# Two gates of the first pair as seven half-wide products, h's sums from x brought again, attention's last blocks earlier

## The chip, the cores and the metric

The kernel runs on one core of one Trainium2 chip. The metric is the device time of one execution in microseconds, the median of several runs.

## The reference

One layer of a hybrid encoder trunk, batch 1, sequence S = 512, D = 2048, float32 in and out. `x` is normalised (RMSNorm with a gain) to `h`; one projection `z = h @ W_in` feeds four mixers: A a gated MLP over blocks of 128 positions, B sliding-window attention (8 query heads, 2 key/value heads, width 64, chunks of 64), C trailing means, D a gated convolution of 31 taps. Each mixer is projected to D and multiplied by a sigmoid gate of `h`. An output projection, a residual, and a SwiGLU with its own norms follow.

```python
h = rms_norm(x, norm_mix_pre[l])
z = h @ w_in[l]
...
merged = jax.nn.sigmoid(h @ w_gate[l, 0] + b_gate[l, 0]) * y_a
merged = merged + jax.nn.sigmoid(h @ w_gate[l, 1] + b_gate[l, 1]) * y_b
merged = merged + jax.nn.sigmoid(h @ w_gate[l, 2] + b_gate[l, 2]) * y_c
merged = merged + jax.nn.sigmoid(h @ w_gate[l, 3] + b_gate[l, 3]) * y_d
x = x + rms_norm(merged @ w_o[l], norm_mix_post[l])
h2 = rms_norm(x, norm_ffn_pre[l])
gu = h2 @ w_ffn_in[l]
f = (jax.nn.silu(gu[..., :D_FF]) * gu[..., D_FF:]) @ w_ffn_out[l]
x = x + rms_norm(f, norm_ffn_post[l])
```

## The kernel before, in words

**Layout and precision.** Activations lie transposed: features on the 128 partitions in tiles, the 512 positions along the free dimension. Every matrix product is made of float16 matmuls on a high and a low part of both factors, three matmuls for one: high x high, high x low, low x high. ScalarE makes the high part of a weight unit by a Copy (`hi`, L630), VectorE the low part as weight minus high part (`lo`, L1121). A unit is 128x1024 weights (512 KB), brought by SP into one of 8 stage slots; the two parts go to one of 4 ring slots (`wq`). So `load(q)` waits until the low part of the unit that had the stage slot is made, and `hi(u)` waits until the products of the unit four before are done. The normalisation factor of `h` is applied after the product, when a bank is emptied, so `h` itself is stored as x times the gain in two float16 parts.

**Order of the work.** There are 13 chunks of W_in (n = 0 to 12; four units each, 52 in all; from chunk 2 on they are copied as a whole, `hi_chunk` L638 and `lo_chunk` L1128). A chunk is two output tiles, each of two units and 48 matmuls of 512 columns. Then come the gates: eight pairs jj of output tiles, and in each pair four gates j = 0 to 3 for the branches D, B, A, C. Behind each gate's product stands the branch's own projection (`branch`, one unit, 24 matmuls; for C six), and VectorE's `merge` multiplies it by the sigmoid and adds up. Every engine runs its own instruction stream in the order in which the code is written; semaphores join them.

**Plain gates and product gates.** A plain gate is two tiles of two units (`plain_tile`, L1969 to L1971). It is used for pair 0, for all four j. Pairs 1 to 7 use Strassen's scheme: four quarter units of weights and their sums (`make_s3`, `make_s2`, `make_s1`, `make_s4` on VectorE) give seven products of half width (`product`, L1976 to L1978: 24 matmuls of 256 columns each) into banks Q1 to Q4. ScalarE keeps three of the results (`keep_product`, L826), VectorE adds them (`c22_c21` L1159 and L1160, `c12_c11`), and the next products wait for these by `copied` and `c_read`.

**The sums of h.** The products need four sums of quarters of `h` for each of the eight pairs of tiles (`tset`). `h_sums(i)` adds the two float16 parts of the pair again (L1500, 128x1024), then makes four steps of 128x256 (L1169 to L1175), ScalarE takes the high part (`t_high`, L787) and VectorE the low part (`h_t_low`, L1179). Two buffers `t_h` take turns. In pair 0 the sums of tiles 0 to 2 are made in gate j=0, 3 to 5 in j=1, 6 and 7 in j=2. TensorE waits for `t_lo` = 8 before the first product gate.

**Tasks.** Small work is hung between the big products by a number k: `tasks(2n)` and `tasks(2n+1)` of chunk n on ScalarE and VectorE; TensorE does task 2n+1 after the first tile of chunk n and task 2n+2 after the second. Gates j = 0 to 3 go on with k = 26 to 33. Attention has four blocks m of 128 positions: scores (TensorE), softmax (VectorE: maximum, shift), exponentials (ScalarE, L694), normalisation (VectorE, L1295 to L1303), transposes of the probabilities (TensorE), their high and low part, heads (TensorE), high and low part of the result (`heads_high` L710, `heads_low` L1323). The tables are

```python
SCORES_AT, NORMALIZE_AT, PROBS_AT, HEADS_AT = (15, 17, 20, 23), (15, 18, 21, 24), (16, 19, 22, 25), (17, 20, 23, 26)
```

Tasks 20 to 23 also transpose the values of mixer A through bank 7, one block of positions each; `value_stats(m)` on VectorE (L1366 to L1370) empties the bank and counts `av_used`, on which the next transposes wait. Task 22 makes the low part of the convolution's output (`d_out`, L1408), task 27 the spatial gating (L1426, L1429) after 16 matmuls (L2190), tasks 27 and 31 the windows of mixer C (L1436), which GpSimd sums (L570 to L578), tasks 28 and 29 the parts of `a_out`, tasks 32 and 33 those of `c_out`. In the gates ScalarE's order for plain gate j is: hi of B+4 and B+5, sigmoid of tile 0 (L800), hi of B+6 and B+7, sigmoid of tile 1 (L809), hi of B+8, where B = `U_G0 + 5*j` is the gate's first unit, B+4 its branch and B+5 the next gate's first. `U_G0` is unit 52.

## Time and profile before

| what | value |
|---|---|
| median of 3 runs | 2445.07 us (2444.79 to 2445.9) |
| the profiled execution | 2445.74 us, its span 2444.0 us |
| TensorE busy | 2422.7 us |
| VectorE busy | 2103.2 us |
| ScalarE busy | 1169.2 us |
| granted TensorE clock | 0.999 |

In the profile's names PE is TensorE, DVE VectorE, ACT ScalarE, POOL GpSimd and SP SyncE, which issues all DMAs. The span is shorter than the execution's time by what lies around it. In a timeline the first number is the start in us from the span's start, the second the duration, and in brackets stands how long the engine had been idle and what released it. Matmuls are pipelined: the duration of one (0.38 us) is longer than the distance to the next, so a group's price is read from the distance between starts. The granted clock stays at its upper level (2.4 GHz) through the span.

### The profile page before, as it was taken

What the parts mean: (1) busy time and instruction counts of PE and PEld (TensorE: products, weight loads), DVE (VectorE), ACT (ScalarE), POOL (GpSimd) and SP (SyncE); (2) the same over time, 40 slices, a digit from 0 to 9 for tenths busy, and PEclk for the clock granted to TensorE, in tenths of its full rate; (3) what the DMA queues carried; (4) which work ended last, traced back from release to release, by engine and by line L of the source; (5) the groups of instructions that cost most, each with busy time, mean ns of one, the idle gap of its engine ahead of it and who ended that gap; (6) DMA issues with size and microseconds to landing.
All of it is one profiled execution on the core that took longest, in us unless ns stands there. A gap on an engine that the chain in (4) does not pass through costs nothing.

```text
span 2444.0 us, 45875 instructions
## 1 busy us (share of the span) xinstructions
PE 2422.7 (99%) x19471; PEld 1893.2 (77%) x19471; DVE 2103.2 (86%) x2292; ACT 1169.2 (48%) x1409; POOL 117.9 (5%) x91
## 2 busy tenths in 40 slices
PE   9999999999999999999899999999999999999998
PEld 5444446888888888768648888888888888888887
DVE  7997588788888888898898999999999998777776
ACT  5235234444444444456564555555555554444443
POOL 0000020000000000011310000000000000000011
PEclk9999999999999999999999999999999999999999
DMA  6222222323333333334333433433433346433436
GB/s 261 104 104 104 73 84 92 120 98 122 114 102 125 106 123 105 132 147 148 113 129 113 138 129 120 138 129 120 138 129 120 137 152 252 143 119 122 136 113 251
DMA packets 97210, 317.94 MB, mean 130 GB/s; under 512 B 9504, under 2 KB 26272, under 8 KB 95648
## 3 DMA queue, kind: packets, MB, share of 16 engines
q1 hardware_dynamic: 97056, 315.81, 37.4%
q8 instruction: 106, 1.74, 0.3%
q14 instruction: 48, 0.39, 0.0%
HBM read 292.18 MB, written 23.59 MB: 129 GB/s over the span
## 4 chain that ended last, share of the span: by engine, by line
PE 88%; DVE 8%; issue 2%; ACT 1%; DMA 1%; POOL 0%; DVEq 0%; SPq 0%; ACTq 0%; POOLq 0%
PE psum L1976 17%; PE psum L1977 17%; PE psum L1978 17%; PE psum L1969 7%; PE psum L1971 7%; PE psum L1970 7%; PE psum L2323 5%; PE psum L2324 5%; PE psum L2325 5%; DVE wq L1121 2%; DVE region_f L1351 1%; DVE region_f L1669 1%; ACT wq L630 1%; DVE region_f L1478 0%; DVE region_f L1489 0%
## 5 line engine op out<-in xcount | busy, mean ns | idle before, releaser
L630 ACT ACTIVATE wq<-stage 128x1024 f16<-128x1024 f32 (+1 forms) x758 | 776.4, 1030 | 685.3 <-DVE stage L1144 277.7
L1121 DVE SCALAR_TENSOR_TENSOR wq<-stage,wq 128x1024 f16<-128x1024 f32 (+1 forms) x758 | 901.4, 1199 | 234.1 <-ACT wq L630 229.5
L1976 PE MATMUL psum<-region_t,wq 128*128 128x256 f16 x2368 | 645.5, 273 | 0.0
L1977 PE MATMUL psum<-region_t,wq 128*128 128x256 f16 x2368 | 645.5, 273 | 0.0
L1978 PE MATMUL psum<-region_t,wq 128*128 128x256 f16 x2368 | 645.5, 273 | 0.0
L1976 PE MATMUL psum<-region_f,wq 128*128 128x256 f16 x1776 | 484.1, 273 | 2.1 <-DVE work L1159 1.8
L1978 PE MATMUL psum<-region_f,wq 128*128 128x256 f16 x1776 | 484.1, 273 | 0.0
L1977 PE MATMUL psum<-region_f,wq 128*128 128x256 f16 x1776 | 484.1, 273 | 0.0
L1969 PE MATMUL psum<-region_f,wq 128*128 128x512 f16 x720 | 272.9, 379 | 0.9 <-DVE wq L1121 0.9
L1970 PE MATMUL psum<-region_f,wq 128*128 128x512 f16 x720 | 272.9, 379 | 0.0
L1971 PE MATMUL psum<-region_f,wq 128*128 128x512 f16 x720 | 272.9, 379 | 0.0
L1977 PEld LDWEIGHTS psum<-region_t,wq 128*128 128x128 f16 x2368 | 231.7, 98 | 26.9
L1976 PEld LDWEIGHTS psum<-region_t,wq 128*128 128x128 f16 x2368 | 231.7, 98 | 26.9
L1978 PEld LDWEIGHTS psum<-region_t,wq 128*128 128x128 f16 x2368 | 231.7, 98 | 26.7
L2323 PE MATMUL psum<-region_f,wq 128*128 128x256 f16 x873 | 238.0, 273 | 1.3 <-DVE wq L1121 1.3
L2325 PE MATMUL psum<-region_f,wq 128*128 128x256 f16 x873 | 238.0, 273 | 0.0
L2324 PE MATMUL psum<-region_f,wq 128*128 128x256 f16 x873 | 238.0, 273 | 0.0
L826 ACT ACTIVATE work<-psum 128x256 f32<-128x256 f32 x222 | 84.9, 382 | 290.4 <-PE psum L1978 253.3
L1976 PEld LDWEIGHTS psum<-region_f,wq 128*128 128x128 f16 x1776 | 173.8, 98 | 27.4 <-DVE wq L1121 3.6
L1977 PEld LDWEIGHTS psum<-region_f,wq 128*128 128x128 f16 x1776 | 173.8, 98 | 23.1
L1978 PEld LDWEIGHTS psum<-region_f,wq 128*128 128x128 f16 x1776 | 173.8, 98 | 20.0
L1971 PEld LDWEIGHTS psum<-region_f,wq 128*128 128x128 f16 x720 | 70.4, 98 | 85.0
(267 smaller groups left out, 2970.0 us busy)
## 6 DMA issues: line engine op xcount, KB each, us to landing
stage<-w_ffn_in_chunks SPq DMA_DIRECT2D x176, 512.0 KB, 3.8
stage<-w_gate_chunks SPq DMA_DIRECT2D x128, 512.0 KB, 3.7
stage<-w_ffn_out_chunks SPq DMA_DIRECT2D x64, 448.0 KB, 3.7
stage<-w_in_chunks SPq DMA_DIRECT2D x52, 512.0 KB, 5.6
stage<-w_o_chunks SPq DMA_DIRECT2D x32, 512.0 KB, 3.8
stage<-w_ffn_out_chunks SPq DMA_DIRECT2D x32, 512.0 KB, 3.8
stage<-w_branch_chunks SPq DMA_DIRECT2D x24, 512.0 KB, 3.5
t_spill<-region_f SPq DMA_DIRECT2D x22, 512.0 KB, 3.2
```

The costliest lines, as they stand in the source:

```text
L630: nc.scalar.activation(dst, stage[:, SLOT[q], 0:UNIT_W[u]], ACT.Copy, scale=WSCALE).then_inc(hi_ready, 1)
L826: nc.scalar.activation(copies[:, i, :], psum[:, Q1, 0:HS], ACT.Copy).then_inc(copied, 1)
L1121: V.scalar_tensor_tensor(out=slot[:, 1, 0:w], in0=stage[:, SLOT[q], 0:w], scalar=WSCALE, in1=slot[:, 0, 0:w], op0=ALU.mult, op1=ALU.subtra ...
L1969: mm(to, w[:, 0, w_at:w_at + P], x_hi, start=start, stop=False)
L1970: mm(to, w[:, 0, w_at:w_at + P], x_lo, start=False, stop=False)
L1971: return mm(to, w[:, 1, w_at:w_at + P], x_hi, start=False, stop=stop)
L1976: mm(to, w[:, 0, w_at:w_at + P], x[:, 0, :], start=start, stop=False, skip_group_check=True)
L1977: mm(to, w[:, 0, w_at:w_at + P], x[:, 1, :], start=False, stop=False, skip_group_check=True)
L1978: return mm(to, w[:, 1, w_at:w_at + P], x[:, 0, :], start=False, stop=stop, skip_group_check=True)
L2323: mm(to, w[:, 0, i * P:i * P + P], xi[:, 0, :], start=first and i == 0, stop=False, skip_group_check=True)
L2324: mm(to, w[:, 0, i * P:i * P + P], xi[:, 1, :], start=False, stop=False, skip_group_check=True)
L2325: done = mm(to, w[:, 1, i * P:i * P + P], xi[:, 0, :], start=False, stop=last and i == n - 1, skip_group_check=True)
```

## The change

- In pair 0 only gates j = 0 and 1 stay plain (`PLAIN_G = 2`); j = 2 and 3 become product gates, with the weights' quarters in that order. All product gates are counted anew by `gate_at`. TensorE waits for `t_lo` = 8 before pair 0's gate j=2.
- `h_sums` no longer adds the two parts of `h`. SP brings the pair of tiles of `x` again into a buffer (`bring_pair`), ScalarE multiplies it in place by the gain (`pair_scaled`), and VectorE makes the four steps from it. Five places serve as buffers for the eight pairs; they lie in the regions of the values, the keys and a free part.
- The sums are made earlier: 0 in chunk 11, 1 to 3 in chunk 12, 4 and 5 in gate j=0, 6 and 7 in gate j=1.
- Attention's blocks 2 and 3 are moved up: scores at 20 and 22, normalisation in the same tasks, probabilities at 21 and 23, heads at 22 and 24. For even tasks ScalarE's exponentials move from `tasks` ahead of the chunk's weight copy.
- Mixer C's last two windows go from task 31 to 29, its high part from 32 to 30, its low part from 33 to 31.

```diff
-PLAIN_O, PLAIN_FFN = 2, 4
+PLAIN_G, PLAIN_O, PLAIN_FFN = 2, 2, 4
...
+def gate_at(jj, j):
+    n = 4 * jj + j - PLAIN_G
+    return U_G + (SU + 1) * n, CS_G + n
...
-SCORES_AT, NORMALIZE_AT, PROBS_AT, HEADS_AT = (15, 17, 20, 23), (15, 18, 21, 24), (16, 19, 22, 25), (17, 20, 23, 26)
+SCORES_AT, NORMALIZE_AT, PROBS_AT, HEADS_AT = (15, 17, 20, 22), (15, 18, 20, 22), (16, 19, 21, 23), (17, 20, 22, 24)
...
-        t_h = view(region_f, O + 2 * b2, 4 * S, F32, "p (u q s) -> p u q s", u=2, q=4)
+        t_h = [view(region_f, i, 2 * S, F32, "p (q s) -> p q s", q=4)
+               for i in (X + 6 * S, O, O + 2 * S, O + 8 * S, O + 10 * S, X + 6 * S, O + 8 * S, O + 10 * S)]
... SP
+            def bring_pair(i):
+                sp.dma_start(t_h[i].rearrange("p (r h) s -> p r (h s)", r=2), x[:, 2 * i:2 * i + 2, :]).then_inc(x_landed[i], 16)
+            def bring_pairs(q):
+                if q == 4 * N_IN + 7:
+                    sp.wait_ge(av_done, NB)
+                    bring_pair(1)
+                    bring_pair(2)
+                    sp.wait_ge(pv_done, NB)
+                    bring_pair(3)
+                    bring_pair(4)
+                if q == 4 * N_IN + 9:
+                    sp.wait_ge(t_lo, 1)
+                    bring_pair(5)
+                if q == 4 * N_IN + 14:
+                    sp.wait_ge(t_lo, 4)
+                    bring_pair(6)
+                if q == 4 * N_IN + 15:
+                    sp.wait_ge(t_lo, 5)
+                    bring_pair(7)
+            sp.wait_ge(h_lo, KT)
+            sp.wait_ge(x_squared, PAIRS)
+            bring_pair(0)
...
                         load(q + i, w_gate[jj, j, i])
+                        bring_pairs(q + i)
... ScalarE
+                if k in SCORES_AT and k % 2 == 0:
+                    exp_part(SCORES_AT.index(k))
...
                     act.wait_ge(au_ready, BT)
+                    act.wait_ge(t_lo, 3)
...
+            def pair_scaled(i):
+                act.wait_ge(x_landed[i], 32)
+                for k in (2 * i, 2 * i + 1):
+                    some = t_h[i][:, 2 * (k % 2):2 * (k % 2) + 2, :]
+                    nc.scalar.activation(some, some, ACT.Copy, scale=vecs[:, V_PRE + k:V_PRE + k + 1]).then_inc(v_made, 1)
...
                 finish(n, 0)
-                if n + 1 == N_IN:
+                if n == N_IN - 1:
+                    act.wait_ge(unit_done, DONE[4 * (N_IN - 2) + 3])
+                    t_high(0)
                     hi(U_G0)
                     hi(U_G0 + 1)
                 attention_highs(2 * n + 1)
                 tasks(2 * n + 1)
+                if n == N_IN - 2:
+                    pair_scaled(0)
+                    pair_scaled(1)
+                if n == N_IN - 1:
+                    pair_scaled(2)
+                    t_high(1)
+                    pair_scaled(3)
                 finish(n, 1)
             hi(U_G0 + 2)
+            t_high(2)
             hi(U_G0 + 3)
... first_gate(j), ScalarE
                 hi(u + 4)
                 col = V_BG + b * KT
+                if j == 0:
+                    pair_scaled(4)
+                    t_high(3)
                 hi(u + 5)
-                if j < 3:
-                    t_high(3 * j)
+                if j == 0:
+                    pair_scaled(5)
+                if j == 1:
+                    t_high(6)
                 act.wait_ge(evicted0, E_G + j + 1)
                 nc.scalar.activation(sig0_0, sig0_0, ACT.Sigmoid, bias=vecs[:, col:col + 1]).then_inc(gate_open, 1)
-                if j < 3:
-                    t_high(3 * j + 1)
                 tasks(k + 1)
+                if j == 0:
+                    t_high(4)
                 hi(u + 6)
+                if j == 0:
+                    pair_scaled(6)
                 hi(u + 7)
-                if j < 2:
-                    t_high(3 * j + 2)
+                if j == 0:
+                    t_high(5)
+                    pair_scaled(7)
+                if j == 1:
+                    t_high(7)
                 act.wait_ge(evicted1, E_G + j + 1)
                 nc.scalar.activation(sig1_0, sig1_0, ACT.Sigmoid, bias=vecs[:, col + 1:col + 2]).then_inc(gate_open, 1)
                 hi(u + 8)
... VectorE, chunk 12
                 if n == N_IN - 1:
+                    h_sums(1)
+                    h_t_low(0)
                     lo(U_G0)
                     lo(U_G0 + 1)
...
+                if n == N_IN - 2:
+                    h_sums(0)
+                if n == N_IN - 1:
+                    h_sums(2)
+                    h_t_low(1)
                 evict(n, 1)
             lo(U_G0 + 2)
+            h_sums(3)
+            h_t_low(2)
             lo(U_G0 + 3)
... VectorE, plain gate j (now for j in range(PLAIN_G))
                 lo(B + 4)
+                if j == 0:
+                    h_sums(4)
+                    h_t_low(3)
+                if j == 1:
+                    h_sums(6)
+                    h_t_low(5)
+                if j == PLAIN_G - 1:
+                    make_s3(U_G, CS_G)
                 lo(B + 5)
...
                 lo(B + 6)
+                if j == 0:
+                    h_t_low(4)
+                    h_sums(5)
+                if j == 1:
+                    h_sums(7)
+                    h_t_low(6)
+                if j == PLAIN_G - 1:
+                    make_s2(U_G, CS_G)
+                    make_s1(U_G, CS_G)
                 lo(B + 7)
+                if j == 1:
+                    h_t_low(7)
... VectorE, product gate
+                if jj == 0:
+                    tasks(2 * (N_IN + j))
...
                 scale_gate(1, 3 * cs + 2)
+                if jj == 0:
+                    tasks(2 * (N_IN + j) + 1)
... TensorE
+                    u, cs = gate_at(0, j)
+                    pe.wait_ge(t_lo, KP)
+                    strassen(h, u, cs, cs == 0)
```

## Rows read from the trace of the kernel before

**Rows 1.** The page: busy time of each engine, and one costly group.

```profile
PE 2422.7 (99%) x19471; PEld 1893.2 (77%) x19471; DVE 2103.2 (86%) x2292; ACT 1169.2 (48%) x1409; POOL 117.9 (5%) x91
...
L630 ACT ACTIVATE wq<-stage 128x1024 f16<-128x1024 f32 (+1 forms) x758 | 776.4, 1030 | 685.3 <-DVE stage L1144 277.7
```

**Rows 2.** What TensorE waited for: us in total, times, longest.

```profile
PE psum L1976 <- DVE work L1159: 1.8, 7, 0.7
```

**Rows 3.** Busy time of each engine in one stretch.

```profile
80.00:398.00 318.00, 318.00 (x1722) 151.31 (x1720) 257.88 (x298) 117.50 (x105) 24.56 (x26) 1.00 0.26 92
```

**Rows 4.** TensorE's timeline, first matmuls of groups, and a last one.

```profile
295.65 0.39 PE L1969 MATMUL psum<-region_f,wq 128*128 128x512 f16 x1
...
309.60 0.38 PE L1969 MATMUL psum<-region_f,wq 128*128 128x512 f16 x1
...
376.94 0.38 PE L1969 MATMUL psum<-region_f,wq 128*128 128x512 f16 x1
...
398.95 0.27 PE L1976 MATMUL psum<-region_f,wq 128*128 128x256 f16 x1
...
414.56 0.27 PE L1978 MATMUL psum<-region_f,wq 128*128 128x256 f16 x1
```

**Rows 5.** VectorE's timeline, tasks 20 to 22.

```profile
228.00 0.69 DVE L1323 TENSOR_TENSOR region_f<-psum,region_f 128x512 f16<-128x512 f32 x1 [1.18 <-ACT region_f L710]
...
231.28 0.69 DVE L1366 BATCH_NORM_STATS2 lnstat<-psum 128x6 f32<-128x512 f32 x1
...
232.88 4.42 DVE L1128 SCALAR_TENSOR_TENSOR region_t<-stage,region_t 128x4096 f16<-128x4096 f32 x1
...
239.01 1.21 DVE L1295 TENSOR_REDUCE rms<-region_t 128x8 f32<-128x1024 f32 x1
...
241.84 0.69 DVE L1366 BATCH_NORM_STATS2 lnstat<-psum 128x6 f32<-128x512 f32 x1
...
252.64 2.28 DVE L1408 TENSOR_TENSOR region_f<-region_f 128x2048 f16<-128x2048 f32 x1
254.84 0.69 DVE L1366 BATCH_NORM_STATS2 lnstat<-psum 128x6 f32<-128x512 f32 x1
```

**Rows 6.** ScalarE's timeline, tasks 20 and 21.

```profile
231.49 1.28 ACT L694 ACT_TABLE_LOAD   x1
...
233.96 1.28 ACT L733 ACT_TABLE_LOAD   x1
...
241.07 1.52 ACT L733 ACTIVATE region_f<-region_f,vecs 128x512 f32<-128x512 f32 x2
242.63 1.91 ACT L738 ACTIVATE region_f<-region_f 128x2048 f16<-128x2048 f32 x1
```

**Rows 7.** ScalarE's groups from 1225 to 1290 us: busy us, mean ns of one.

```profile
L948 ACT ACTIVATE region_f<-region_f,vecs 128x512 f32<-128x512 f32 x16 | 10.4, 708 | 2.5 <-DVE region_t L1179 2.5
```

**Rows 8.** Four loads of SP, issued from 237.3 to 238.7 us.

```profile
DMA to landing us min/median/max: 3.6/5.1/6.4
```

**Rows 9.** VectorE's timeline from chunk 12's end to the end of gate j=0.

```profile
295.59 2.35 DVE L1121 SCALAR_TENSOR_TENSOR wq<-stage,wq 128x1024 f16<-128x1024 f32 x2
...
303.34 1.22 DVE L1500 TENSOR_TENSOR region_f<-region_f 128x1024 f32<-128x1024 f16 x1
304.59 0.43 DVE L1169 TENSOR_TENSOR region_f<-region_f 128x256 f32<-128x256 f32 x1
...
313.23 0.68 DVE L1426 TENSOR_TENSOR region_f<-psum,region_f 128x512 f32<-128x512 f32 x1
...
318.53 1.29 DVE L1436 SCALAR_TENSOR_TENSOR region_f<-work,region_f 128x512 f32<-128x512 f32 x2
...
322.97 1.29 DVE L1169 TENSOR_TENSOR region_f<-region_f 128x256 f32<-128x256 f32 x1
...
328.29 2.05 DVE L1121 SCALAR_TENSOR_TENSOR wq<-stage,wq 128x1024 f16<-128x1024 f32 x1
```

**Rows 10.** GpSimd's timeline, its third window.

```profile
319.82 2.03 POOL L572 TENSOR_TENSOR work<-region_f 128x511 f32<-128x511 f32 x1
```

More of the change, by code:

```diff
@@ L119 @@
     plain_units((UW,) * 4)
-for b in BRANCHES:
-    plain_units((UW,) * 4 + ((2 * P,) if b == 2 else (UW,)))
-for jj in range(1, PAIRS):
+def gate_at(jj, j):
+    n = 4 * jj + j - PLAIN_G
+    return U_G + (SU + 1) * n, CS_G + n
+for jj in range(PAIRS):
     for j, b in enumerate(BRANCHES):
-        strassen_units(CS_G + 4 * (jj - 1) + j)
+        if jj == 0 and j < PLAIN_G:
+            plain_units((UW,) * 4)
+        else:
+            assert len(UNIT_AT) == gate_at(jj, j)[0]
+            strassen_units(gate_at(jj, j)[1])
         plain_units((2 * P,) if b == 2 else (UW,))
@@ L412, in _ @@
                         load(q + 4, w_branch[jj, j if j < 3 else 0])
+                    bring_pairs(q + 4)
                     q += 5
@@ L724, in tasks @@
                     mean_root(psum[:, 7, :], BW, LN_EPS, var_done, 1, cstd_ready)
-                if k in SCORES_AT:
+                if k in SCORES_AT and k % 2:
                     exp_part(SCORES_AT.index(k))
@@ L810, in first_gate @@
                 hi(u + 8)
-            for j in range(4):
+            for j in range(PLAIN_G):
                 first_gate(j)
@@ L847, in gate @@
                 hi(u + 11)
-            for jj in range(1, PAIRS):
-                for j in range(4):
+            for jj in range(PAIRS):
+                for j in range(0 if jj else PLAIN_G, 4):
                     gate(jj, j)
@@ L1437, in tasks, with h_sums, h_t_low @@
                                                in1=c_x[:, g, :], op0=ALU.mult, op1=ALU.subtract).then_inc(win_used, 1)
-                if k == 33:
+                if k == 31:
                     dve.wait_ge(c_hi, 1)
                     V.tensor_tensor(c_out[:, :, 1, :], c_x[:, :, :], c_out[:, :, 0, :], ALU.subtract).then_inc(c_lo, 1)
+            def h_sums(i):
+                dve.wait_ge(v_made, 2 * i + 2)
+                sum_halves(t_h[i], (0, 2, 1, 3))
+            def h_t_low(i):
+                dve.wait_ge(t_hi, i + 1)
+                V.tensor_tensor(by_half(tset[:, :, i, 1, :]), by_tile(t_h[i]), by_half(tset[:, :, i, 0, :]),
+                                ALU.subtract).then_inc(t_lo, 1)
             for n in range(1, N_IN):
@@ L1490, in merged_low @@
                                     merged[:, :, t, jj, 0, :], ALU.subtract).then_inc(m_lo, 1)
-            def h_sums(i):
-                t = t_h[:, i % 2]
-                if i == 0:
-                    dve.wait_ge(b_lo, NB)
-                    dve.wait_ge(h_lo, KT)
-                elif i >= 2:
-                    dve.wait_ge(t_lo, i - 1)
-                V.tensor_tensor(t.rearrange("p (h r) s -> p h r s", h=2), h[:, :, :, i, 0, :], h[:, :, :, i, 1, :],
-                                ALU.add).then_inc(dve_step, 1)
-                dve.wait_ge(dve_step, step.up())
-                sum_halves(t)
-            def h_t_low(i):
-                t_low(i, t_h[:, i % 2], i + 1)
-            for j in range(4):
+            for j in range(PLAIN_G):
                 B, k = U_G0 + 5 * j, 2 * (N_IN + j)
@@ L1588, in gate @@
                 merge(jj, j, u + SU, (cb[:, 0, :], cb[:, 1, :]))
-            for jj in range(1, PAIRS):
-                for j in range(4):
+            for jj in range(PAIRS):
+                for j in range(0 if jj else PLAIN_G, 4):
                     gate(jj, j)
@@ L2252, in _ @@
             for j in range(4):
[L2253 to L2260 removed]
+                n = N_IN + j
+                if j < PLAIN_G:
+                    u = U_G0 + 5 * j
+                    pe.wait_ge(evicted0, E_G + (0, 1, 0)[j])
+                    plain_tile(u, 0, h, wq, bank=GATE_BANK[j])
+                    tasks(2 * n + 1)
+                    pe.wait_ge(evicted1, E_G + (0, 1, 0)[j])
+                    plain_tile(u + 2, 1, h, wq, bank=GATE_BANK[j])
+                    tasks(2 * n + 2)
+                    u += 4
+                else:
+                    u, cs = gate_at(0, j)
+                    pe.wait_ge(t_lo, KP)
+                    strassen(h, u, cs, cs == 0)
+                    u += SU
+                pe.wait_ge(lo_ready, u + 1)
                 if j == 1:
@@ L2269, in _ @@
                     pe.wait_ge(y_used, 2 * j)
-                branch(u + 4, j, 0)
-            def pair_stage(jj, first=False):
+                branch(u, j, 0)
+            for jj in range(1, PAIRS):
                 for j in range(4):
-                    u, cs = U_G + GU * (jj - 1) + (SU + 1) * j, CS_G + 4 * (jj - 1) + j
-                    strassen(h, u, cs, first and j == 0)
+                    u, cs = gate_at(jj, j)
+                    strassen(h, u, cs)
                     pe.wait_ge(lo_ready, u + SU + 1)
@@ L2278, in pair_stage @@
                     branch(u + SU, j, jj // 2)
-            pe.wait_ge(t_lo, KP)
-            pair_stage(1, first=True)
-            for jj in range(2, PAIRS):
-                pair_stage(jj)
             for c in range(PLAIN_O):
```

68 lines of the change are left out of this document (25 added, 43 removed).

## The prediction

> **What bounds the kernel now.** I read the page first. TensorE is busy 2422.7 us of 2444.0 [rows 1]; the reader is to see that only what shortens or interrupts TensorE's queue can change the time. The waits of TensorE come next: among them VectorE holds it 1.8 us in seven waits for the reading of C21, the longest 0.7 and the other six 0.2 each [rows 2]. Then I cut out the stretch that the change rewrites: from 80 to 398 us TensorE is busy all of it [rows 3], no wait stands there. So the change can win only matmul time and that 0.7 us wait, and it can lose wherever its new order makes TensorE wait. After that I read TensorE's timeline for the pitch of its matmuls [rows 4], and those of VectorE, ScalarE and GpSimd, operation by operation [rows 5 to 10], because with no wait of today to read from, each new one has to be walked.
>
> **1. The matmuls.** Gate j=3 of pair 0 starts at 376.94 and has 96+6 matmuls of 512 columns up to 398.95: 22.01/102 = 0.2158 us each [rows 4]. The first six products after it are 144 matmuls of 256 columns, the first starting at 398.95 and the last at 414.56: 15.61/143 = 0.1092 us [rows 4]. A gate of four plain units is 96 x 0.2158 = 20.72 us, one of seven products 168 x 0.1092 = 18.35. Two gates give back 4.75 us, all on the path, at either end if nothing waits.
>
> **2. The first product gate's wait.** Today the longest of the seven waits sits in pair 1, gate 0, where VectorE has also the merged tile's low part (two instructions, 1.2 us) between it and C21. The first product gate is now pair 0's j=2, with no merged tile, so its 0.7 goes and pair 1 joins the six at 0.2: 0.5 us gained (bounds: 0, if VectorE comes late into j=2 as walked below, and 0.7).
>
> **3. Attention's blocks 2 and 3 moved up.** TensorE's work is the same, in other places. What is new is that VectorE does softmax and normalisation in one task, waits for ScalarE's exponentials between them, and has d_out's low part and value_stats behind them. I walk from the end of chunk 10's second tile (t = 0).
> TensorE: heads, scores and transposes of task 22 take what they take today in task 20 (2.16 us up to 227.85); the first tile of chunk 11 48 x 0.2158 = 10.36; eight transposes of the probabilities 0.88. At t = 13.4 it comes to the transposes for value_stats(3), which wait until value_stats(2) has emptied bank 7.
> The other side: in task 20 block 2's exponentials end at 233.96 as today [rows 6], but then come normalisation (2.8), value_stats (1.6) and chunk 11's low part (4.4) [rows 5] before VectorE evicts chunk 10's first tile at 242.7, some 4.5 after that tile's end. ScalarE waits for it with the first GELU, then has block 2's copy (1.0), SiLU (table load 1.28 [rows 6], two instructions 1.52), d_out's copy (1.91) [rows 6] and the load for the next GELU, and is there at t = 1.1. GELU and heads_high 1.2 bring it to 2.3; heads_low and softmax 231.28-228.00 = 3.3 [rows 5] to 5.65; table load and exponentials 233.96-231.49 = 2.5 [rows 6] to 8.2; normalisation 241.84-239.01 = 2.8 [rows 5] to 11.0; d_out's low part 254.84-252.64 = 2.2 to 13.2; value_stats 232.88-231.28 = 1.6 and its last write 0.1 [rows 5] to 14.9. TensorE waits 14.9 + 0.1 - 13.4 = **1.6 us**. Bounds: 0.3 if the table load is done before the wait, about 2.6 if ScalarE is a further microsecond late. Behind that wait are all of chunks 11 and 12, so it is lost for good. The same walk for block 2 in task 20 ends 0.7 us before TensorE asks: nothing.
>
> **4. h's sums.** Removed are eight adds of 128x1024 on VectorE (1.22 each) [rows 9]; they end no wait of today, so they give nothing by themselves. Added are 16 scalings on ScalarE; the nearest row is the same operation of the FFN, 0.71 each [rows 7], two in 1.35. Added too are eight DMAs of 512 KB. SP's queue is in order: pair 6 is issued behind the load of unit 66, which waits for the low part of B+6 (B: gate 0's first unit, 52), and pair 7 behind load 67, which waits for that of B+7. ScalarE has pair 6's scaling before the high part of B+7, and pair 7's before sigmoid 1 and the high part of B+8. So ScalarE waits for two DMAs that hang on its own previous step. Four loads issued in 1.4 us land between 3.6 and, for the last, 6.4 after its issue [rows 8]: one alone 3.6, each further (1.4+6.4-3.6)/3 = 1.4. A pair issued behind a load lands 5.0 after that load's issue.
> Walk from the start of gate j=0 (g = 0, 295.65 today [rows 4]). TensorE: first tile 10.4, gMLP's 16 matmuls to 309.60 today, so 13.95 [rows 4]; B+2 done at 19.1, second tile at 24.3, branch at 29.5; gate j=1 at 50.2, its branch at **55.4**. Then it wants product gate j=2, which first waits for all eight low parts of the sums (t_lo = 8).
> The chain: VectorE has task 27 from 14.15 on, 318.53-313.23 = 5.3, and 1.2 for two windows: 20.65. Low part of B+6 (1.15 back to back, two took 2.35 [rows 9]): 21.8. Pair 6 landed 26.85; scaled 28.2; high part of B+7 (1.03 [rows 1]) 29.2, low part 30.4; pair 7 landed 35.4; scaled 36.8; sigmoid 37.5; high part of B+8 38.5; gMLP's copy (1.9, as d_out's [rows 6]) 40.4; high part of gate j=1's branch 41.4. From there VectorE is the bound: eight operations of 128x1024 at 1.14 (four low parts of weights, three of sums, S3) 9.1; two h_sums of 1.8 (four steps of 0.43 and the wait between them [rows 9]) 3.6; scaling 0.6, gMLP's low part 2.2 (as 252.64 [rows 5]) and two windows 1.2; S2 and S1, each on the one before, 2.5. Together 19.2: t_lo = 8 at 60.7. TensorE waits **5.3 us**, behind it the whole rest of the kernel. Lower bound 0: had ScalarE not waited for pairs 6 and 7, VectorE would start these 19.2 us at 36.0 (unit done 34.7, copy 1.0) and end at 55.3, just in time. Upper bound below.
> Pairs 0 to 5 cost nothing: with their waits in SP (h_lo and x_squared long met, then av_done, pv_done, t_lo) SP has issued pair 4 about 7 us before the low part of unit 52 lets load 60 go, and ScalarE needs load 60 only some 50 us on. Without that cover each would delay the loads behind it one for one. On ScalarE pair 1's scaling waits for its DMA (behind the four loads that chunk 12's low part sets free, 5.0 + 3 x 1.4 after it) and holds heads_high(3), t_high(0) and the high part of unit 52 behind it; the last comes 1 us after unit 48 is done, and TensorE needs it 15 us later.
>
> **5. c_out in gate j=2.** Its low part (2.2 us) stands behind the gate's first scaling. A gate with a 5.2 us branch has 23.5 us of TensorE and about 19 of VectorE, so it fits; 0, bound +1.
>
> **Sum**: -4.75 - 0.5 + 1.6 + 5.3 = +1.65 us, for the profiled execution 2445.74 + 1.65 = 2447.4. It lies 0.67 above the median of the runs, so the forecast is 2445.07 + 1.65 = **2446.7 us**: no change to be told, as 0.2% (4.9 us) is about what a measurement can tell.
>
> **The rivals.** *A: the pairs come in time* (ScalarE has other slack than I count, or x lands sooner). Only the 1.6 is left: 2445.07 - 5.25 + 1.6 = 2441.4. For it: the walk without these waits ends level with TensorE. Against it: two full round trips of 5.0 us in series. Chance 0.17. *B: no new wait at all*: 2445.07 - 5.25 = 2439.8, faster. It needs value_stats(2) early too, 1.5 us against a walk of rows. 0.09.
> *C: GpSimd holds VectorE's sums up*, on the other side. While GpSimd ran its windows (an add at 319.82 took 2.03 [rows 10]), an h_sums step took 1.29 where it took 0.43 before, and a low part 2.05 where 1.22 [rows 9]. Now h_sums(3) falls into GpSimd's first windows (4 x 0.86 = 3.4 us, of which 1.5 are idle before task 27: 1.9 left), and the low parts of B+6 and B+7 into the second (0.83 each): 3.6 more on the chain, and 0.5 for the first window's scaling: wait 9.4, time 2446.7 + 4.1 = 2450.8. It is slower by over 0.2% from 3.3 us of such delays on. Chance 0.17; against it, the two low parts at 295.59 took 2.35 beside GpSimd's first windows, undisturbed [rows 9]. The Trainium skill (SBUF — State Buffer, "SBUF: two separate sides") says that a VectorE operation with two SBUF inputs and a GpSimd operation that reads SBUF lock each other out for a whole instruction; this trace agrees in the 1.29. By that rule each of h_sums' steps could wait for a whole 2.03 us add, and the time would be rival C's or above.
>
> **How the numbers follow.** Forecast 0.57 (own range 2444.5 to 2449), A 0.17, B 0.09, C 0.17. The range 2441.0 to 2450.8 reaches from A to C's centre, leaving out B (0.09) and the upper half of C (0.08). Faster by over 0.2% is B, 0.09; slower is C, 0.17; the rest 0.74.
>
> **What would show it.** Right: the two gates' 512-column matmuls become 336 of 256 at 0.109; TensorE idle about 1.6 us before the transposes for value_stats(3), released by VectorE's value_stats; ScalarE idle twice, about 5 us each, before the scalings of pairs 6 and 7, released by DMA; TensorE idle about 5 us before gate j=2, released by the low part of a sum. Wrong: no idle at gate j=2 (A), or h_sums' steps of 1.3 us around it (C). The likeliest error is the landing time of the pairs: each microsecond counts twice, once for pair 6 and once for pair 7.

## The result and the profile after

The changed kernel takes 2450.11 us (median of 19 runs, 2448.53 to 2451.57), the kernel before 2445.78 beside it (19 runs, 2444.60 to 2447.01): ratio 1.0019, 95% interval [1.0012, 1.0025]. It is 4.3 us slower. The forecast was 2446.7, inside a range of 2441.0 to 2450.8, with no change to be told as the likeliest case. The ratio lies at that case's edge: its middle is under 0.2%, a part of its interval above. The sum said +1.65 us; 2.7 us of loss are not in it. The time also lies 1.1 us above 2449, where the forecast's own case ended: the range holds it only because it was drawn up to the centre of rival C.

The profiled execution took 2450.26 us. Its page, first the span and the busy time of each engine, answers to [rows 1]:

```profile
span 2448.5 us, 46237 instructions
PE 2420.8 (99%) x19615; PEld 1904.2 (78%) x19615; DVE 2113.5 (86%) x2304; ACT 1188.0 (49%) x1437; POOL 116.4 (5%) x91
```

TensorE is busy 1.9 us less than before and the span is 4.5 longer, so what was lost stands in its waits. Its waits, us in total, times and the longest, answer to [rows 2]:

```profile
PE psum L2060 <- DVE region_t L1523: 6.2, 1, 6.2
...
PE psum L2266 <- DVE region_f L1444: 1.4, 1, 1.4
...
PE psum L2060 <- DVE work L1232: 1.3, 7, 0.2
```

Two are new. L1523 makes the low part of h's sums, and TensorE waits for the last of the eight before gate j=2. L1444 is value_stats, before the transposes for value_stats(3). The seven waits for C21 are left with 0.2 each. The same stretch as [rows 3], and then four smaller ones around gate j=2 (from:to, length, busy us of TensorE and its weight loads, VectorE, ScalarE, GpSimd, then the granted clock, the busy share of the DMA engines and what they moved in GB/s):

```profile
80.00:398.00 318.00, 310.30 (x1819) 161.54 (x1818) 260.58 (x301) 132.87 (x130) 23.06 (x26) 0.99 0.28 101
...
352.30:356.30 4.00, 0.00 (x0) 0.00 (x0) 3.97 (x5) 1.31 (x2) 0.00 (x0) 1.00 0.00 0
...
356.40:358.50 2.10, 0.00 (x0) 0.00 (x0) 2.10 (x3) 0.60 (x1) 0.00 (x0) 0.50 0.00 0
...
358.50:363.10 4.60, 4.55 (x22) 3.25 (x23) 2.87 (x4) 3.46 (x3) 0.00 (x0) 0.50 0.02 4
...
363.10:370.00 6.90, 6.90 (x65) 6.13 (x64) 5.11 (x6) 2.85 (x5) 0.00 (x0) 0.99 0.30 92
```

Of 318 us, 7.7 are idle: the two new waits. VectorE is busy in all of the long one. The granted clock tells what no list of waits does: it falls from 1.00 to 0.50 (from 2.4 to 1.2 GHz) some 4 us into the wait and is back only at 363.2, after 22 matmuls. TensorE's timeline there (start, duration, instruction):

```profile
358.55 0.39 PE L2060 MATMUL psum<-region_f,wq 128*128 128x256 f16 x1 [6.25 <-DVE region_t L1523]
358.73 0.42 PE L2061 MATMUL psum<-region_f,wq 128*128 128x256 f16 x1
...
363.21 0.27 PE L2061 MATMUL psum<-region_f,wq 128*128 128x256 f16 x1
```

The 22 matmuls from 358.55 to 363.21 take 4.66 us; at 0.1092 each [rows 4] it would be 2.40. That is 2.25 us of matmuls at half the clock, which count as busy. The Trainium skill (TensorE: Matmul & The Clock Gate, "Part 1: The HAM clock gate (the "warmup" mystery)") says that an idle TensorE goes back to half its clock and recovers only when it has been busy again; this trace agrees in the 0.50 of the two windows and the 0.99 behind them.

No later slack takes the 2.25 us back. The 16 matmuls of gMLP in gate j=0 (kernel before, then after) and pair 1's first product give the count:

```profile
306.03 3.73 PE L2190 MATMUL psum<-region_f 128*128 128x128 f32 x32
```
```profile
307.12 3.73 PE L2274 MATMUL psum<-region_f 128*128 128x128 f32 x32
...
403.97 0.27 PE L2060 MATMUL psum<-region_f,wq 128*128 128x256 f16 x1
```

TensorE is 1.1 us late in gate j=0, and at pair 1's first product 403.97 - 398.95 [rows 4] = 5.0: 1.1, 6.4 for the wait from start to start, 2.25 for the clock, less the 4.75 of the matmuls.

What made the wait long is in ScalarE's timeline (in brackets the idle time ahead, and what ended it):

```profile
316.13 1.06 ACT L672 ACTIVATE wq<-stage 128x1024 f16<-128x1024 f32 x1 [3.06 <-PE psum L2055]
325.18 1.33 ACT L818 ACTIVATE region_f<-region_f,vecs 128x512 f32<-128x512 f32 x2 [7.99 <-DMA region_f<-x_t]
326.42 1.04 ACT L672 ACTIVATE wq<-stage 128x1024 f16<-128x1024 f32 x1
...
333.83 1.33 ACT L818 ACTIVATE region_f<-region_f,vecs 128x512 f32<-128x512 f32 x2 [5.42 <-DMA region_f<-x_t]
```

and in SP's: each x_t is a pair brought right behind a load of weights, which had itself waited for VectorE.

```profile
319.04 0.33 SPq L404 DMA_DIRECT2D stage<-w_branch_chunks  x1
319.41 1.50 SPq L420 DMA_DIRECT2D region_f<-x_t  x1
328.78 0.33 SPq L404 DMA_DIRECT2D stage<-w_gate_chunks  x1
329.15 0.43 SPq L420 DMA_DIRECT2D region_f<-x_t  x1
```

Pair 6 is there 325.18 - 319.04 = 6.1 us after the load ahead of it was issued, pair 7 333.83 - 328.78 = 5.05. SP spent 1.50 us on issuing pair 6, and 0.43 on pair 7. VectorE's timeline shows the two ends of the chain, and GpSimd's effect in between:

```profile
317.79 1.22 DVE L1194 SCALAR_TENSOR_TENSOR wq<-stage,wq 128x1024 f16<-128x1024 f32 x1
318.93 2.06 DVE L1523 TENSOR_TENSOR region_t<-region_f,region_t 128x1024 f16<-128x1024 f32 x1
...
321.35 1.14 DVE L1245 TENSOR_TENSOR region_f<-region_f 128x256 f32<-128x256 f32 x1
322.53 1.28 DVE L1247 TENSOR_TENSOR region_f<-region_f 128x256 f32<-128x256 f32 x1
...
327.49 1.26 DVE L1194 SCALAR_TENSOR_TENSOR wq<-stage,wq 128x1024 f16<-128x1024 f32 x1 [3.20 <-ACT wq L672]
...
336.75 1.23 DVE L1194 SCALAR_TENSOR_TENSOR wq<-stage,wq 128x1024 f16<-128x1024 f32 x1 [7.40 <-ACT wq L672]
...
339.50 1.23 DVE L1194 SCALAR_TENSOR_TENSOR wq<-stage,wq 128x1024 f16<-128x1024 f32 x1 [0.32 <-ACT wq L672]
...
357.27 1.22 DVE L1523 TENSOR_TENSOR region_t<-region_f,region_t 128x1024 f16<-128x1024 f32 x1
```

While GpSimd had its windows, a low part took 2.06 instead of 1.2 and two steps of a sum 1.14 and 1.28 instead of 0.43. Behind them VectorE is idle 3.20 us, so that cost nothing. The low part at 327.49 is another matter, for load 67 waits for it. When it began, the GpSimd add below was still running, and the low part ended 1.08 us after that add (e7 shows what this is worth):

```profile
326.64 1.03 POOL L614 TENSOR_TENSOR work<-work 128x508 f32<-128x508 f32 x1
```

From 339.50 to the end of the last low part VectorE works without a gap: 19.0 us.

### The profile page after: what moved, and what is told of

Same layout as the page of the kernel before. It is cut to its first block, busy times and chain, and to the rows that moved or that the text cites. A ratio compares the mean times of both kernels' runs of the same rounds, so it can differ in the third digit from the quotient of the medians.

```text
span 2448.5 us, 46237 instructions
## 1 busy us (share of the span) xinstructions
PE 2420.8 (99%) x19615; PEld 1904.2 (78%) x19615; DVE 2113.5 (86%) x2304; ACT 1188.0 (49%) x1437; POOL 116.4 (5%) x91
## 4 chain that ended last, share of the span: by engine, by line
PE 81%; DVE 13%; issue 3%; ACT 2%; DMA 1%; POOL 0%; DVEq 0%; SPq 0%; ACTq 0%; POOLq 0%
PE psum L2060 17%; PE psum L2062 17%; PE psum L2061 17%; PE psum L2410 5%; PE psum L2412 5%; PE psum L2411 5%; PE psum L2053 5%; PE psum L2055 5%; PE psum L2054 5%; DVE wq L1194 3%; ACT wq L672 1%; DVE region_f L1425 1%; DVE region_f L1753 1%; DVE stage L1217 1%; DVE stage L1222 1%
## 5 line engine op out<-in xcount | busy, mean ns | idle before, releaser
L2062 PE MATMUL psum<-region_t,wq 128*128 128x256 f16 x2432 | 663.3, 273 | 0.0
L2061 PE MATMUL psum<-region_t,wq 128*128 128x256 f16 x2432 | 663.2, 273 | 0.0
L2060 PE MATMUL psum<-region_t,wq 128*128 128x256 f16 x2432 | 663.2, 273 | 0.0
L2060 PE MATMUL psum<-region_f,wq 128*128 128x256 f16 x1824 | 498.5, 273 | 7.8 <-DVE region_t L1523 6.2
L2062 PE MATMUL psum<-region_f,wq 128*128 128x256 f16 x1824 | 498.5, 273 | 0.0
L2061 PE MATMUL psum<-region_f,wq 128*128 128x256 f16 x1824 | 498.5, 273 | 0.0
L2060 PEld LDWEIGHTS psum<-region_t,wq 128*128 128x128 f16 x2432 | 237.5, 98 | 28.0
L2062 PEld LDWEIGHTS psum<-region_t,wq 128*128 128x128 f16 x2432 | 237.5, 98 | 28.0
L2061 PEld LDWEIGHTS psum<-region_t,wq 128*128 128x128 f16 x2432 | 237.5, 98 | 27.9
L2053 PE MATMUL psum<-region_f,wq 128*128 128x512 f16 x656 | 249.4, 380 | 1.5 <-DVE wq L1194 1.5
L2055 PE MATMUL psum<-region_f,wq 128*128 128x512 f16 x656 | 249.4, 380 | 0.0
L2054 PE MATMUL psum<-region_f,wq 128*128 128x512 f16 x656 | 249.4, 380 | 0.0
L2410 PE MATMUL psum<-region_f,wq 128*128 128x256 f16 x873 | 238.1, 273 | 1.5 <-DVE wq L1194 1.5
L2412 PE MATMUL psum<-region_f,wq 128*128 128x256 f16 x873 | 238.1, 273 | 0.0
L2411 PE MATMUL psum<-region_f,wq 128*128 128x256 f16 x873 | 238.1, 273 | 0.0
L2060 PEld LDWEIGHTS psum<-region_f,wq 128*128 128x128 f16 x1824 | 178.5, 98 | 35.0 <-DVE region_t L1523 6.7
L2061 PEld LDWEIGHTS psum<-region_f,wq 128*128 128x128 f16 x1824 | 178.5, 98 | 24.4
L2062 PEld LDWEIGHTS psum<-region_f,wq 128*128 128x128 f16 x1824 | 178.5, 98 | 21.4
L2055 PEld LDWEIGHTS psum<-region_f,wq 128*128 128x128 f16 x656 | 64.2, 98 | 77.8 <-issue 0.6
```

Source lines behind the costliest of these rows:

```text
L2053: mm(to, w[:, 0, w_at:w_at + P], x_hi, start=start, stop=False)
L2054: mm(to, w[:, 0, w_at:w_at + P], x_lo, start=False, stop=False)
L2055: return mm(to, w[:, 1, w_at:w_at + P], x_hi, start=False, stop=stop)
L2060: mm(to, w[:, 0, w_at:w_at + P], x[:, 0, :], start=start, stop=False, skip_group_check=True)
L2061: mm(to, w[:, 0, w_at:w_at + P], x[:, 1, :], start=False, stop=False, skip_group_check=True)
L2062: return mm(to, w[:, 1, w_at:w_at + P], x[:, 0, :], start=False, stop=stop, skip_group_check=True)
```

## The experiments

All times are medians beside the kernel before on the same chip: 2445.47 us for e1, e2, e3 and e5, 2445.49 for e4, e6 and e7, 2446.24 for e8 and e9. So times of different groups, and of the changed kernel with its 2445.78, are compared to within 0.8 us only.

**e1: both pairs one load earlier.** The rest is the changed kernel.

```diff
-                if q == 4 * N_IN + 14:
+                if q == 4 * N_IN + 13:
                     sp.wait_ge(t_lo, 4)
                     bring_pair(6)
-                if q == 4 * N_IN + 15:
+                if q == 4 * N_IN + 14:
                     sp.wait_ge(t_lo, 5)
                     bring_pair(7)
```

> SP issues pair 6 of x behind load 65 and pair 7 behind load 66, one load earlier each. If the two DMA round trips on ScalarE's chain made the 6.2 us wait before gate j=2: pair 6 lands near 315, before ScalarE asks; pair 7 is let go by the fifth low part of the sums (about 321) and lands near 325, 9 us sooner than 333.8; VectorE ends the eight low parts about when TensorE asks, the wait is under 1 us, the clock stays up there, and the time falls by 6 + 2.3 = 7 to 8.5 us, to 2442 to 2443. Rival (VectorE's own work, or GpSimd's lock, is the bound): the wait stays above 4 us and the time above 2447.

Measured: 2442.05 us, ratio 0.9986 [0.9977, 0.9995]. TensorE goes into gate j=2 without a wait and at full clock, and the wait for value_stats stays, at 1.46. ScalarE finds pair 7 landed, and the window around the gate's start is full (columns as above):

```profile
325.50 1.32 ACT L818 ACTIVATE region_f<-region_f,vecs 128x512 f32<-128x512 f32 x2
```
```profile
345.00:363.00 18.00, 18.00 (x133) 12.87 (x132) 14.90 (x18) 9.19 (x10) 0.00 (x0) 1.00 0.11 37
```

It follows that the long wait and the fall of the clock hang on the two round trips in series: with them out of the chain nothing is left of either.

**e5: only pair 6 earlier**, the first two changed lines of e1's diff.

> Only pair 6 is issued a load earlier, pair 7 stays behind load 67. If the two round trips stand in series: ScalarE makes the high part of B+7 at 322.5 in place of 327.5, but VectorE's low part of it waits for the steps of the fifth sums until 324.5, so pair 7 lands near 330.5 in place of 333.8; 3.3 us come off the chain, the wait before gate j=2 falls from 6.2 to about 3, and whether the clock still falls there shows how long an idle stretch it takes in this kernel: 2450.1 - 3.3 = 2446.8 with the fall, 2444.5 without. Rival (only the last DMA counts, pair 6's is hidden): no change.

Measured: 2447.32 us, ratio 1.0007 [0.9998, 1.0016], which tells no difference from before. The wait before gate j=2 is 3.5, so each of the two round trips carries its part. The clock fell all the same, from 355.1 on, and the first 29 matmuls ran at 0.50:

```profile
PE psum L2060 <- DVE region_t L1523: 3.5, 1, 3.5
```
```profile
355.90:362.00 6.10, 6.07 (x29) 4.33 (x30) 4.26 (x6) 4.20 (x5) 0.00 (x0) 0.50 0.23 73
```

**e2: d_out's low part ahead of the softmax in VectorE's task 22.** It is moved from behind `normalize` to before it, so VectorE does it while ScalarE computes exponentials.

```diff
+                if k == 22:
+                    dve.wait_ge(d_hi, 1)
+                    V.tensor_tensor(d_out[:, :, 1, :], conv[:, :, :], d_out[:, :, 0, :], ALU.subtract).then_inc(d_lo, 1)
                 if k in NORMALIZE_AT:
                     normalize(NORMALIZE_AT.index(k))
...
-                if k == 22:
-                    dve.wait_ge(d_hi, 1)
-                    V.tensor_tensor(d_out[:, :, 1, :], conv[:, :, :], d_out[:, :, 0, :], ALU.subtract).then_inc(d_lo, 1)
```

> d_out's low part (2.28 us on VectorE) goes ahead of block 3's normalisation, into the 2.56 us in which VectorE waits for the exponentials. If it stood in the way of value_stats(2): the 1.4 us wait of TensorE before the transposes for value_stats(3) is gone. The gain arrives at the end only if the 6.2 us wait before gate j=2 does not grow by it: its chain starts from TensorE's own units, so it should move along, and the time falls by 1.4 us. Rival: the chain is tied to the pairs' DMAs alone, the wait before gate j=2 grows by what the first gave, and the time stays.

Measured: 2448.60 us, ratio 1.0013 [1.0004, 1.0022], 1.5 less than the changed kernel and 1.2 less when each is taken beside its own kernel before. TensorE is busy in all of 80 to 340 us, and the wait before gate j=2 stays:

```profile
80.00:340.00 260.00, 260.00 (x1453) 124.92 (x1452) 212.47 (x249) 109.37 (x101) 23.08 (x26) 1.00 0.30 108
```
```profile
PE psum L2060 <- DVE region_t L1523: 6.1, 1, 6.1
```

In this trace SP issued pair 6 in 0.43 us, and the low part of B+7 took 1.78 beside a GpSimd add (SP, VectorE, GpSimd):

```profile
318.19 0.33 SPq L404 DMA_DIRECT2D stage<-w_branch_chunks  x1
318.56 0.43 SPq L420 DMA_DIRECT2D region_f<-x_t  x1
```
```profile
326.13 1.78 DVE L1194 SCALAR_TENSOR_TENSOR wq<-stage,wq 128x1024 f16<-128x1024 f32 x1 [2.67 <-ACT wq L672]
```
```profile
325.80 1.03 POOL L614 TENSOR_TENSOR work<-work 128x508 f32<-128x508 f32 x1
```

**e4: attention's move alone**, in the kernel before: the four tables, and the exponentials of even tasks in `attention_highs`.

```diff
-SCORES_AT, NORMALIZE_AT, PROBS_AT, HEADS_AT = (15, 17, 20, 23), (15, 18, 21, 24), (16, 19, 22, 25), (17, 20, 23, 26)
+SCORES_AT, NORMALIZE_AT, PROBS_AT, HEADS_AT = (15, 17, 20, 22), (15, 18, 20, 22), (16, 19, 21, 23), (17, 20, 22, 24)
...
+                if k in SCORES_AT and k % 2 == 0:
+                    exp_part(SCORES_AT.index(k))
...
-                if k in SCORES_AT:
+                if k in SCORES_AT and k % 2:
                     exp_part(SCORES_AT.index(k))
```

> The kernel before with attention's blocks 2 and 3 moved up as in the change, and nothing else. If the wait before the transposes for value_stats(3) comes from softmax and normalisation in one task with d_out's low part behind them: TensorE waits 1.3 to 1.6 us there, before task 23, and the time rises by that, to about 2447.3. Rival (it needs the pairs' DMAs or the sums too): no wait and no change.

Measured: 2447.54 us, ratio 1.0011 [1.0002, 1.002]. It is 2.05 us slower than before, and 1.5 of that is the wait, there with nothing else changed and released by the same operation:

```profile
PE psum L2184 <- DVE region_f L1372: 1.5, 1, 1.5
```

**e3: e1 and e2 together.**

> Both edits. If the two waits are independent: the sum, 2450.1 - 8 - 1.4 = about 2440.7, 5 us under the kernel before, which is the matmuls' 4.75 and the 0.5 of the first product gate's wait. If they are not, it lies with the pairs' edit alone.

Measured: 2440.14 us, ratio 0.9978 [0.9969, 0.9987]: faster than the kernel before and the changed one. On the same chip as e1 and 1.9 us faster, it shows e2's edit once more. The whole stretch is full again, and it now reaches further into the product gates (1908 matmuls where [rows 3] has 1722). The last low part of the sums, begun at 348.97, is done just before TensorE comes to gate j=2 at 350.46:

```profile
80.00:398.00 318.00, 318.00 (x1908) 169.37 (x1907) 270.63 (x312) 139.48 (x137) 24.16 (x26) 1.00 0.29 105
```
```profile
348.97 1.22 DVE L1523 TENSOR_TENSOR region_t<-region_f,region_t 128x1024 f16<-128x1024 f32 x1
```

**e6: TensorE kept at work in the wait.** The changed kernel with 28 float32 matmuls on the identity, results unused, ahead of the wait for t_lo; the trace records each as two.

```diff
                     u, cs = gate_at(0, j)
+                    if cs == 0:
+                        keep_clock(28)
                     pe.wait_ge(t_lo, KP)
```

> The changed kernel with 28 small matmuls (128x128 float32, about 5.3 us) put on TensorE ahead of its wait for the eight low parts, in the idle stretch before gate j=2. They compute nothing that is used. The wait itself stays (the gate starts at 358.5), but the granted clock should not fall from 356.4 to 363.2: the first 22 matmuls of the gate run 0.109 apart in place of 0.213, 2.3 us less, time about 2447.8. Rival (the slow matmuls are hidden, because VectorE's c22_c21 is the bound in that gate anyway): the clock stays up and the time too is as without, 2450.1.

Measured: 2448.86 us, ratio 1.0013 [1.0004, 1.0022]. The clock stays up. TensorE's timeline has the filler and the gate's first matmul, the window has the gate's first 50 matmuls at full clock:

```profile
351.77 6.41 PE L2087 MATMUL psum<-ident,ones 128*128 128x128 f32 x56
358.02 0.27 PE L2060 MATMUL psum<-region_f,wq 128*128 128x256 f16 x1
```
```profile
357.80:363.00 5.20, 5.20 (x50) 4.67 (x49) 3.46 (x6) 4.54 (x5) 0.00 (x0) 1.00 0.08 9
```

The gate starts 358.02 - 351.77 = 6.25 us after the filler began, so the wait's length is unchanged. The profiled execution took 2447.99 us, 2.3 under that of the changed kernel, but it was the fastest of its 11 runs. The medians differ by 1.25, by 1.0 beside the kernels before, and the intervals of the two ratios overlap. That the matmuls lose 2.25 us and that filler prevents it is shown in the traces; the runs alone don't settle its price. That the slow matmuls are not hidden, as this run's rival had it, rests on pair 1's start at 403.97 above.

**e7: GpSimd's windows left out.** The changed kernel with one memset for each window in place of its copies and adds, so mixer C's windows are zero and its result is not the reference's.

```diff
-                    nc.gpsimd.tensor_copy(dst[:, 0:d], src[:, 0:d]).then_inc(pool_step, 1)
-                    step.up()
-                    last = nc.gpsimd.tensor_tensor(dst[:, d:S], src[:, d:S], src[:, 0:S - d], ALU.add)
-                    last.then_inc(pool_step, 1)
+                    if k < g:
+                        continue
+                    nc.gpsimd.memset(dst, 0.0).then_inc(pool_step, 1)
```

> The changed kernel in which GpSimd leaves out mixer C's window sums (one memset for each window stands in place of its copies and adds, so branch C's result is not the reference's). Theory: GpSimd's slowing of VectorE falls into VectorE's idle time, since the DMAs set the chain: the wait before gate j=2 stays at 5.5 to 6.2 us, the time within 1 us of 2450.1. Rival C of the prediction (GpSimd's lock is on the chain): the wait falls by 2 us or more.

Measured: 2449.06 us, ratio 1.0015 [1.0006, 1.0024]. The wait shrinks from 6.25 to 4.96, by 1.3 and not by the 2 or more that rival C wanted. The lines that answer to the chain above (VectorE, then SP):

```profile
PE psum L2059 <- DVE region_t L1522: 5.0, 1, 5.0
```
```profile
318.42 1.24 DVE L1522 TENSOR_TENSOR region_t<-region_f,region_t 128x1024 f16<-128x1024 f32 x1
...
320.06 0.42 DVE L1244 TENSOR_TENSOR region_f<-region_f 128x256 f32<-128x256 f32 x1
```
```profile
318.53 0.33 SPq L404 DMA_DIRECT2D stage<-w_branch_chunks  x1
318.90 0.43 SPq L420 DMA_DIRECT2D region_f<-x_t  x1
```

VectorE's operations are at 1.24 and 0.42 again, and the 2.4 us that they took longer with GpSimd at work had gone into idle time. Nor did the wait stay at 5.5 to 6.2, as I had expected: 1.3 us of GpSimd's work were on the chain. Where they were is seen beside the other traces in which pair 6 stands behind load 66 (us; the last two columns from the issue of load 66):

| kernel | issue of pair 6 | low part of B+7 | pair 6 there | load 67 issued |
|---|---|---|---|---|
| changed | 1.50 | 1.26 | 6.1 | 9.74 |
| e6 | 1.70 | 1.57 | 5.8 | 9.75 |
| e2 | 0.43 | 1.78 | 5.6 | 9.75 |
| e7 | 0.43 | 1.23 | 5.4 | 8.99 |

With GpSimd's windows load 67 goes out at the same moment however long SP's issue took and whenever pair 6 landed: the low part ends 1.08 us after the same GpSimd add (327.67, 327.33 and 326.83), so an earlier pair 6 only made it longer. Without them it goes out 0.75 earlier. Load 66 itself is 0.4 earlier in its gate, since VectorE is not held up in GpSimd's first windows, and pair 7 lands 0.15 sooner after load 67: together 1.3.

**e9: e3 with GpSimd's windows left out** in the same way, so mixer C's result is again not the reference's.

> The version with both edits, in which GpSimd leaves out mixer C's window sums (one memset for each window, so branch C's result is not the reference's). Without them the changed kernel's wait before gate j=2 was 5.0 in place of 6.2 us. If GpSimd counts only through the chain of pairs 6 and 7, which is gone here: no wait before gate j=2 with or without it, the time stays at 2440.1 within 0.7. Rival (it slows VectorE on the way to the end elsewhere in this stretch): 1 us or more less.

Measured: 2440.61 us, ratio 0.9977 [0.9968, 0.9987], the same as e3. Where the pairs are off the chain, GpSimd's work costs nothing that can be measured.

**e8: the sums added from h's two parts again.** The kernel of e3 without `bring_pair` and `pair_scaled`; VectorE adds as before the change, the sums' places are the new ones.

```diff
-                dve.wait_ge(v_made, 2 * i + 2)
+                if i == 0:
+                    dve.wait_ge(h_lo, KT)
+                else:
+                    free, n = (av_done, av_done, pv_done, pv_done, t_lo, t_lo, t_lo)[i - 1], (NB, NB, NB, NB, 1, 4, 5)[i - 1]
+                    dve.wait_ge(free, n)
+                V.tensor_tensor(by_tile(t_h[i]), h[:, :, :, i, 0, :], h[:, :, :, i, 1, :], ALU.add).then_inc(dve_step, 1)
+                dve.wait_ge(dve_step, step.up())
```

> The version with both edits (pairs earlier, d_out's low part first), in which h_sums again adds the two parts of h on VectorE (1.22 us each) and x is neither brought again nor scaled; the sums keep their new places. If the second bringing of x earns its keep only through VectorE: in gate j=1 VectorE has no idle time to spare (the eighth low part ends 0.1 us before TensorE asks), the adds of sums 6 and 7 put 2.3 to 2.5 us on it, TensorE waits about 2.3 us before gate j=2 and the time is 2442.4, or up to 2445 if the clock falls there as well. Rival (the adds hide in VectorE's idle time, bringing x again was for nothing): 2440.1, no wait.

Measured: 2447.99 us, ratio 1.0007 [0.9998, 1.0016]. The wait before gate j=2 is 5.6 and not the 2.3 expected: I had charged only the two adds of gate j=1, 2.5 us, but those of the sums before hold up gate j=0 too. The low part with which VectorE's last run of work begins is at 334.61 here, and at 331.09 in e3 (e8, then e3):

```profile
PE psum L2020 <- DVE region_t L1483: 5.6, 1, 5.6
```
```profile
334.61 1.22 DVE L1148 SCALAR_TENSOR_TENSOR wq<-stage,wq 128x1024 f16<-128x1024 f32 x1 [0.32 <-ACT wq L644]
```
```profile
331.09 1.23 DVE L1194 SCALAR_TENSOR_TENSOR wq<-stage,wq 128x1024 f16<-128x1024 f32 x1 [1.73 <-ACT wq L672]
```

So bringing x again, once its two late pairs are moved, is worth 1.0007 - 0.9978 = 0.29%, some 7 us.

**All of them in one sum.** Take 2445.47 - 4.75 - 0.5 = 2440.2 (rival B's terms), add the two waits as each trace shows them, and half the time for which the granted clock was 0.50 with matmuls running:

| kernel | value_stats | before j=2 | clock | sum | median |
|---|---|---|---|---|---|
| e3 | 0 | 0 | 0 | 2440.2 | 2440.14 |
| e1 | 1.5 | 0 | 0 | 2441.7 | 2442.05 |
| e5 | 1.5 | 3.5 | 3.0 | 2448.2 | 2447.32 |
| e6 | 1.5 | 6.25 | 0 | 2447.9 | 2448.86 |
| e7 | 1.5 | 5.0 | 1.6 | 2448.2 | 2449.06 |
| e2 | 0 | 6.1 | 2.7 | 2449.0 | 2448.60 |
| changed | 1.5 | 6.25 | 2.25 | 2450.2 | 2450.11 |

Each agrees within 1.0 us, over a spread of 10. The waits are alike from run to run, but the clock's column is read from one execution of each kernel, and it differs more between kernels than their waits do.

## Why the forecast held, and what its sum lacked

The measured time is inside the range, but above the forecast's own case (up to 2449). The new waits stand where they were walked; the sum was too small by one term that its own case put at nothing, GpSimd's share, and by one that it didn't have, the clock.

**1. The matmuls, -4.75: right.** e3 is 5.3 us under its kernel before, where this term and the next give 5.25.

**2. The reading of C21, -0.5: right.** Seven waits, 1.3 in total, the longest 0.2.

**3. Attention moved up, +1.6: right.** 1.45 in the profile after, 1.5 in e4 where it stands alone, released by value_stats as the walk had it. e2 removes it and the median falls by 1.2 to 1.5, e3 is 1.9 under e1.

**4. h's sums, +5.3: right in its mechanism, short by 0.95 in the wait.** Both of ScalarE's waits for a DMA are there, in series, with the scaling of pair 6 before the high part that sets pair 7's load free; e1 and e5 show that each is needed. Counted as in the walk from gate j=0's start, which is 10.38 us ahead of gMLP's matmuls (295.65 to 306.03 before, so 296.74 in the changed kernel and 296.62 in e7):

| | walked | changed | e7 |
|---|---|---|---|
| low part of B+6 done, load 66 issued | 21.8 | 22.3 | 21.9 |
| pair 6 landed | 26.85 | 28.4 | 27.3 |
| low part of B+7 done, load 67 issued | 30.4 | 32.0 | 30.9 |
| pair 7 landed | 35.4 | 37.1 | 35.8 |
| VectorE's last run starts | 41.4 | 42.8 | 41.5 |
| it takes | 19.2 | 19.0 | 19.0 |
| TensorE is there | 55.4 | 55.6 | 55.6 |

Without GpSimd's windows the walk comes out within 0.1 us at the start of VectorE's last run, so what it lacked is GpSimd's 1.3. The prediction named the landing of the pairs as its likeliest error, each microsecond counting twice. Pair 6 did land 1.1 later behind its load than walked, but that did not set the time: e2, where it landed 0.5 sooner, still has a wait of 6.1.

**The term that is missing: the fall of the clock, +2.25.** The prediction priced a wait at its own length. A wait this long also halved the pace of what followed, and by the traces that is the larger part of the error: 0.95 + 2.25 - 0.15 (step 3) = 3.05 over the sum's 1.65, so 4.7 by terms, where the profiled executions differ by 2450.26 - 2445.74 = 4.5 and the medians by 4.3.

**5. c_out's low part in gate j=2, 0: right**; e3 and e1, which keep it, show no wait there.

**The rivals.** *A and B* did not happen in the changed kernel, but small edits of it make their cases: e1 is A's at 2442.05 (A: 2441.4), e3 is B's at 2440.14 (B: 2439.8), both beside a kernel before of 2445.47, where the rivals were worked out from 2445.07. *C* gave 2450.8, nearer to the 2450.11 measured than my own 2446.7, and still is not what happened. Its mechanism was there at a third of its size: e7 takes GpSimd's work away, and of C's 4.1 us on the chain 1.3 go while 4.96 of the 6.25 us of wait remain; the rest of its slowed operations fell into the 3.20 of idle time before 327.49. In e9 the same edit of the repaired kernel changes nothing. The rest of the way to C's time was the clock, which C did not have: that its number came near was luck. The Trainium skill's rule of the lock between VectorE and GpSimd (SBUF — State Buffer, "SBUF: two separate sides") is borne out: the low part of B+7 began beside a running GpSimd add in the changed kernel, e6, e2 and e5, took 1.26, 1.57, 1.78 and 2.06, and ended 1.08 to 1.09 us after that add each time. Each operation waited for what was left of one add, at most about 1 us here; none had to wait for a whole 2.03 us. A time that fits is no proof of the mechanism that gave it.

What stays open: what makes an issue of SP long now and then. It is not GpSimd's windows: e2 has them in the same place and SP issued pair 6 in 0.43, and in e7, without them, one issue of gate weights took 1.72.

## What to carry to other kernels

In a queue kept in order, a transfer put behind a load inherits what that load waits for; when its consumer stands ahead of the work that sets the next load free, the round trips add up. Moving two such transfers one load forward cost nothing here and was worth 7.8 us with the clock, each kernel beside its own kernel before (4.33 slower, then 3.42 faster). When a walk ends in a new wait of TensorE, ask how long it is: here one of 6.25 us cost about 2.25 more in the matmuls behind it, and one of 1.45 cost only itself. When an engine's slowed operations fall into its idle time, look for the one that doesn't: here a single low part passed GpSimd's delay on, because a load waited for it. And where an engine waits between two halves of a task, look for work that stands behind it in the same task and can go between them, as d_out's low part did in e2 for 1.5 us.

## What the runs showed of the hardware

- Before gate j=2, TensorE's granted clock went from 1.00 to 0.50 during idle times of 6.25, 6.1, 5.6, 5.0 and 3.5 us, and before value_stats(3) it stayed up through those of 1.5. It stayed at 0.50 until 363.2 in the profile after and for at least 6 us of matmuls in e5: the shorter wait was followed by the longer slow stretch (22 matmuls against 29), so the price of a fall doesn't follow from the length of the wait.
- The clock also fell where no wait was longer than 2.0 us: around the merged tiles in the next stage, once or twice in the profiles of the changed kernel, e1, e3, e4, e7, e8 and e9. In those of the kernel before, e2, e5 and e6 it stayed at 1.00 beside waits of the same length (1.8, 0.6 and 2.0 in most). What decides it is not shown here. In the profile after it cost nothing in the end: with it TensorE is late, and the next wait for VectorE, 1.54 us in the trace before, is gone. The window there:

```profile
1213.00:1216.50 3.50, 3.50 (x10) 1.28 (x9) 3.40 (x3) 0.52 (x1) 3.27 (x3) 0.52 0.64 217
```

- SP's issue of one load of gate weights took 0.33 us in the median, but in every profile a few issues took over 1.0 us; the longest load of weights took 1.65 in the profile after and 1.85 in e6's.
- A VectorE operation of 128x1024 that began beside a running GpSimd add ended 1.08 to 1.09 us after it in four traces, and a step of 128x256 0.28 after it in the profile after (322.49 and 323.81, the adds 322.22 and 323.53).
